# Residual laid into the PSUM accumulators ahead of the output projection, in a two-layer hybrid decoder trunk with routed experts

## The chip, the cores and the metric

One NeuronCore of one Trainium2 chip runs the whole program. The metric is the device time of one execution in microseconds, lower is better. Times of groups of runs are given as their median.

## What is computed

The input x has 256 tokens of 1024 float32 values. There are two layers, each a token mixer and then a channel mixer, with RMS norms ahead and residual additions behind. Cut to what matters:

```python
for layer in range(2):
    h = rms_norm(x, norm_mix_g[layer])
    mix = even_mixer(h, ...) if layer % 2 == 0 else odd_mixer(h, ...)   # both end in  o @ w_out
    x = x + mix
    h = rms_norm(x, norm_ffn_g[layer])
    x = x + hier_moe(h, ...)
```

Layer 0 mixes by differential attention (4 heads, whose outputs are normed once more) and stick-breaking attention (8 heads); layer 1 by attention with a forget gate (16 heads). In the channel mixer each token picks one of 4 groups and two of the 4 experts in it; an expert is `(silu(h @ w_gate) * (h @ w_up)) @ w_down` with three matrices of 1024 x 1024, so 12 MB of weights each, and there are 16 experts in each layer. All weights are float32.

## The kernel before, in words

The kernel is written engine by engine, each in an own program order, and the engines meet at semaphores. The residual stream x lies in SBUF as `x_sb`, 128 tokens by 2 by 1024. Its four quarters (q = 0 to 3) are token tile q // 2 and column half q % 2, 128 x 512 each, the size of one PSUM bank. There are eight banks: banks 0 to 3 are named `ACC`, 4 and 5 `GATE` and `UP`, 6 `Y` (also `O_BANK`), 7 `MISC` (also `SUM_BANK`).

**Attention and its end.** TensorE makes scores, transposes and weighted values for 8 jobs, in banks 0 to 6, and ScalarE copies each output into `oT` (L653), counted by `o_ready`. `exp_done` counts the exponentials that ScalarE has taken out of the score banks. In layer 0 VectorE and ScalarE then find the norms of the first four outputs; TensorE spreads them over the partitions in banks 0 and 1 (L1384) and VectorE multiplies (L1136), counted by `sub_applied`.

**Output projection.** TensorE goes through the four quarters, each with 8 float32 products of 128 x 512 (L1395), which the trace records as two passes each, into banks 2 to 5. After each quarter VectorE adds x to the bank and writes the sum to `x_sb` (L797), counted by `x_mixed`. ScalarE sums the squares (L713). TensorE transposes the quarters of the new x through the identity (L1188) into banks 0 to 3, the first two of them in the middle of the projection; VectorE takes them into `hT` with the norm's gain (L774).

**Router.** TensorE multiplies `hT` with the router's weights, in 8 chunks for each token tile (L1411, 20 columns each), into bank 7 and signals `logits_psum`. Then it copies the four quarters of `x_sb` through the identity into banks 0 to 3 (L1416, with start=True), so that the experts' outputs can be accumulated on the residual there, and waits for `chosen`. Meanwhile VectorE works out the choice of experts in some 20 small instructions (L960 to L992, `chosen_bf`), then makes `fn_low` of the second token tile (L812: the part of the normed rows that the rounded copy `fn_high` leaves out), and only then waits for the ranks, which TensorE makes from `chosen_bf` (L1425). From the ranks come slot numbers (L1000, L1003) and the 0/1 matrix `take` of the first expert (L1044).

**Experts.** For each expert TensorE gathers the tokens (L1435, 8 products of 512 columns), ScalarE takes them out (L725), TensorE transposes (L1445), VectorE takes these out (L1058), and then gate, up and down products follow (L1457, 64 columns by 512, in pairs on both halves of the array), in 6 units of 16 recorded passes for each expert. The output of each expert is scattered onto the accumulators (L1469). After the last one VectorE copies the four banks to `x_sb` (L1169).

**Weights.** SP issues all weight loads from one queue. An expert's weights are six units of 2 MB, in a ring of eight slots and a spare one that overlaps `hn` and `hT`. During attention the first expert's six units are loaded, behind them w_out. After the projection (`out_psum`) SP loads two units of the second expert, after the router (`logits_psum`) a third into the spare slot. Each further load waits until TensorE has used the slot (`unit_used`), in a fixed order; the first such refill waits for the first unit of the first expert.

## Time and profile before

| what | value |
|---|---|
| median of three runs | 1252.6 us |
| the three runs | 1251.89, 1252.60, 1255.09 us |
| the profiled execution, its own time | 1256.46 us |
| its span, from the first to the last instruction | 1254.5 us |
| mean granted TensorE clock, as a share of full | 0.984 |
| TensorE busy with products | 1174.7 us (94%) |
| VectorE, ScalarE, GpSimd busy | 423.6, 189.9, 7.2 us |
| read from HBM | 437.8 MB, 350 GB/s over the span |

Times in the profile are microseconds from the start of the span unless marked ns. Rows name an engine, a line of the kernel (L1395), an operation, what it writes and reads, shapes, and how often (x8). PE is TensorE's products, DVE VectorE, ACT ScalarE, SPq the queue of SP, that issues DMAs. In brackets stands how long the engine was idle before and what ended that. A float32 product appears as two records. PEclk is the clock granted to TensorE: 1.00 is 2.4 GHz, 0.50 is 1.2 GHz. Matmul ends are modelled, and rows that are merged are read from their start.

### The profile page before, as it was taken

How to read it: one execution, taken by the hardware profiler on the slowest of the kernel's cores; microseconds unless marked ns; L12 is line 12 of the kernel's file. 1: busy time of each engine (PE TensorE's matmuls, PEld its weight loads, DVE VectorE, ACT ScalarE, POOL GpSimd, SP SyncE). 2: the span in 40 equal slices, each digit the busy share in tenths (PEclk: the TensorE clock that was granted, in tenths of full speed). 3: DMA queues.
4: the chain of work that ended last, by engine and by line, in shares of the span. 5: the costliest groups of instructions: out<-in, count | busy, mean ns of one | idle time of the engine just before them, and what ended most of it. 6: DMA issues, size and time to landing. Idle time of an engine off the chain costs nothing.

```text
span 1254.5 us, 14037 instructions
## 1 busy us (share of the span) xinstructions
PE 1174.7 (94%) x5694; PEld 560.5 (45%) x5694; DVE 423.6 (34%) x748; ACT 189.9 (15%) x374; POOL 7.2 (1%) x36
## 2 busy tenths in 40 slices
PE   5997899999999999989979999999999999999998
PEld 4994453333333333333369864533333333333333
DVE  3654243232322232222255663433222323222223
ACT  3326210000000000000044242100000100000000
POOL 2000000000000000000000000000000000000000
PEclk9998889999999999999989999899999999999999
DMA  9665047999999999999994450699999999999996
GB/s 329 203 256 201 1 197 314 422 418 431 428 428 428 428 428 427 430 428 427 422 364 158 179 202 1 243 429 411 415 433 427 427 427 432 427 428 427 429 429 270
DMA packets 53904, 439.30 MB, mean 350 GB/s; under 512 B 14192, under 2 KB 14192, under 8 KB 29296
## 3 DMA queue, kind: packets, MB, share of 16 engines
q1 hardware_dynamic: 53872, 438.85, 84.5%
q8 instruction: 22, 0.36, 0.1%
q14 instruction: 10, 0.08, 0.0%
HBM read 437.79 MB, written 1.05 MB: 350 GB/s over the span
## 4 chain that ended last, share of the span: by engine, by line
PE 74%; DMA 17%; DVE 4%; ACT 3%; issue 1%; POOL 1%; DVEq 0%; POOLq 0%; SPq 0%; ACTq 0%
PE bank L1457 42%; DMA ring<-in_moe_w_up 11%; PE bank L1350 8%; DMA ring<-in_moe_w_gate 6%; PE bank L1395 5%; PE bank L1435 4%; PE bank L1469 4%; PE bank L1345 3%; PE bank L1445 1%; ACT attention L629 1%; PE bank L1501 1%; PE bank L1416 1%; PE bank L1188 1%; PE bank L1494 1%; PE bank L1282 1%
## 5 line engine op out<-in xcount | busy, mean ns | idle before, releaser
L1457 PE MATMUL bank<-ring,qkT 128*64 128x512 f32 x2944 | 655.0, 597 | 28.3 <-DMA ring<-in_moe_w_gate 15.5
L1457 PEld LDWEIGHTS bank<-ring,qkT 128*64 128x64 f32 x2944 | 204.8, 137 | 454.3 <-issue 406.6
L1152 DVE TENSOR_SCALAR qkT<-qkT 128x512 f32<-128x512 f32 x32 | 13.7, 428 | 486.4 <-ACT qkT L738 486.4
L1154 DVE RECIPROCAL qkT<-qkT 128x512 f32<-128x512 f32 x32 | 107.3, 3353 | 1.1
L1469 PE MATMUL bank<-qkT 64*128 64x512 f32 x256 | 63.6, 615 | 5.6 <-ACT qkT L743 5.6
L1159 DVE TENSOR_TENSOR qkT<-bank,qkT 128x512 f32<-128x512 f32 x32 | 22.1, 692 | 132.0 <-PE bank L1457 132.0
L743 ACT ACTIVATE qkT<-bank 128x512 f32<-128x512 f32 x32 | 19.1, 597 | 304.3 <-PE bank L1457 304.3
L1395 PE MATMUL bank<-ring,hn 128*128 128x512 f32 x128 | 57.3, 606 | 1.4 <-DVE hn L1136 0.8
L738 ACT ACTIVATE qkT<-bank 128x512 f32<-128x512 f32 x32 | 19.1, 598 | 243.2 <-PE bank L1457 243.2
L920 DVE TENSOR_TENSOR w_low<-ring,w_high 128x2048 fp32r<-128x2048 f32 x22 | 49.4, 2286 | 11.6 <-ACT w_high L586 11.6
L1435 PE MATMUL bank<-fn_high,take 128*128 128x512 f32 x136 | 45.9, 419 | 2.1 <-DVE take L1044 2.1
L741 ACT ACTIVATE qkT<-bank 128x256 f32<-128x256 f32 x32 | 12.3, 383 | 224.2 <-PE bank L1494 224.2
L1435 PE MATMUL bank<-fn_low,take 128*128 128x512 f32 x136 | 42.4, 393 | 0.0
L586 ACT ACTIVATE w_high<-ring 128x2048 fp32r<-128x2048 f32 x22 | 40.7, 1898 | 6.3 <-PE bank L1350 6.3
L1395 PEld LDWEIGHTS bank<-ring,hn 128*128 128x128 f32 x128 | 24.7, 196 | 31.9 <-issue 30.3
L1435 PEld LDWEIGHTS bank<-fn_high,take 128*128 128x128 f32 x136 | 22.9, 188 | 31.3 <-issue 28.2
L1469 PEld LDWEIGHTS bank<-qkT 64*128 64x128 f32 x256 | 22.0, 186 | 30.6 <-issue 15.1
L1350 PE MATMUL bank<-h_high,w_high 128*128 128x256 f32 x224 | 30.9, 291 | 0.0
L725 ACT ACTIVATE qkT<-bank 128x512 f32<-128x512 f32 x34 | 20.3, 597 | 62.8 <-PE bank L1435 62.8
L1457 PE MATMUL bank<-ring_spare,qkT 128*64 128x512 f32 x128 | 29.2, 598 | 0.0
L1350 PE MATMUL bank<-h_high,w_low 128*128 128x256 f32 x224 | 29.2, 283 | 0.0
L1350 PE MATMUL bank<-h_low,w_high 128*128 128x256 f32 x224 | 29.1, 283 | 0.0
(217 smaller groups left out, 898.3 us busy)
## 6 DMA issues: line engine op xcount, KB each, us to landing
ring<-in_moe_w_gate SPq DMA_DIRECT2D x64, 2048.0 KB, 22.2
ring<-in_moe_w_down SPq DMA_DIRECT2D x64, 2048.0 KB, 24.9
ring<-in_moe_w_up SPq DMA_DIRECT2D x56, 2048.0 KB, 24.4
ring_spare<-in_moe_w_up SPq DMA_DIRECT2D x8, 2048.0 KB, 26.5
ring<-in_ab_w_in SPq DMA_DIRECT2D x12, 1024.0 KB, 14.2
ring<-in_c_w_in SPq DMA_DIRECT2D x12, 1024.0 KB, 14.4
ring<-in_ab_w_out SPq DMA_DIRECT2D x2, 2048.0 KB, 15.1
ring<-in_c_w_out SPq DMA_DIRECT2D x2, 2048.0 KB, 15.3
```

The costliest lines, as they stand in the source:

```text
L586: act.activation(w_high[u % 2][:, part, :], win_view(u)[:, part, :], ACT.Copy).then_inc(s.w_high, 1)
L725: act.activation(gathered_sb, MISC[:, :], ACT.Copy).then_inc(s.gather_out, 1)
L738: act.activation(sig, GATE[:, :], ACT.Exp, scale=-1.0).then_inc(s.gate_exp, 1)
L920: tt(w_low[u][:, part, :], win_view(u)[:, part, :], w_high[u % 2][:, part, :].bitcast(F32), ALU.subtract).then_inc(s.w_low, 1)
L1154: nc.vector.reciprocal(sig, sig).then_inc(s.gate_step, 1)
L1159: tt(hid, UP[:, :], sig, ALU.mult).then_inc(s.hid_ready, 1)
L1345: last = mm(bank[j % 2][:, :], x_part[:, c, P * t:P * (t + 1)], w[:, c, :], start=(n == 0 and c == 0), stop=(final and c == NC - 1))
L1350: last = mm(bank[j % 2][:, T * half:T * (half + 1)], w[:, c, col:col + P], x_part[:, c, :], start=(n == 0 and half == 0 and c == 0), stop= ...
L1395: last = mm(bank[2 + q][:, :], oT[:, c, P * t:P * (t + 1)], wout_view(c // SUB)[:, c % SUB, HALF * h:HALF * (h + 1)], start=(c == 0), stop ...
L1435: last = mm(MISC[:, :], take[:, t, side:side + P], part[:, t, HALF * h:HALF * (h + 1)], start=(t == 0 and i == 0 and h == 0), stop=(t == N ...
L1457: last = mm(b[SLOTS * half:SLOTS * (half + 1), :], left(h, k), expert_rhs(slot, k, half), start=(h == 0 and k == 0), stop=(h == 1 and k == ...
L1469: last = mm(ACC[2 * t + half][:, :], giveT[k % 2][r, P * t:P * (t + 1)], y_sb[r, :], start=False, stop=False, skip_group_check=True)
```

## The change

The residual goes into banks 0 to 3 ahead of the output projection, and the projection is accumulated on it there. VectorE copies the sum to `x_sb` where it added. The copies through the identity behind the router are gone, and the transposes of the new x go to banks 4, 5, 6 and again 4. Of the copies, those of quarters 2 and 3 (into banks 2 and 3) are issued after the last exponential has been taken out, in layer 0 ahead of the spreading of the norms, and those of quarters 0 and 1 behind the wait for all attention outputs. The fourth group of transposes waits until VectorE has read the first out of bank 4.

```diff
--- before.py
+++ after.py
@@ -273,6 +273,7 @@
         bank = [ctx.enter_context(nc.psum_tensor(f"bank{i}", [P, COLS], F32)) for i in range(8)]
         ACC, GATE, UP, Y, MISC = bank[0:4], bank[4], bank[5], bank[6], bank[7]
         O_BANK, SUM_BANK = bank[6], bank[7]
+        MIXED_T = [bank[4], bank[5], bank[6], bank[4]]
 
 
         pool_step = sem("pool_step")
@@ -765,14 +766,14 @@
                 own(tt(tmp, tmp, ys, ALU.mult))
                 return stt(ys, tmp, 1.5, ys, ALU.add, ALU.mult)
 
-            def leave_transposed(layer, n, table, groups, first_bank):
+            def leave_transposed(layer, n, table, groups, banks):
 
                 s = layers[layer]
                 for g in groups:
                     t, h = g // 2, g % 2
                     dve.wait_ge(s.ht_psum, 8 * layer + 4 * n + g + 1)
                     tt(hT[:, SUB * h:SUB * (h + 1), P * t:P * (t + 1)],
-                       bank[first_bank + g][:, :].rearrange("p (c t) -> p c t", c=SUB),
+                       banks[g][:, :].rearrange("p (c t) -> p c t", c=SUB),
                        gains(table, layer, h, P), ALU.mult).then_inc(s.ht_ready, 1)
 
             def mix_norm(layer):
@@ -785,16 +786,16 @@
                        ).then_inc(s.hn_ready, 1)
                 if layer == 0:
                     dve.wait_ge(gains_loaded, GAINS)
-                leave_transposed(layer, 0, gain_mix, range(4), 2)
+                leave_transposed(layer, 0, gain_mix, range(4), bank[2:6])
 
             def mixed_and_normed(layer):
 
                 s = layers[layer]
 
-                def add(q):
+                def leave(q):
                     dve.wait_ge(s.out_psum, 4 * layer + q + 1)
                     xq = x_sb[:, q // 2, HALF * (q % 2):HALF * (q % 2 + 1)]
-                    tt(xq, bank[2 + q][:, :], xq, ALU.add).then_inc(s.x_mixed, 1)
+                    nc.vector.tensor_copy(xq, ACC[q][:, :]).then_inc(s.x_mixed, 1)
 
                 def norm(t):
                     xs, ys, tmp = root_x[:, t:t + 1], root_y[:, t:t + 1], root_t[:, t:t + 1]
@@ -812,18 +813,18 @@
                     stt(fn_low[:, t, :], x_sb[:, t, :], root_y[:, t:t + 1],
                         fn_high[:, t, :].bitcast(F32), ALU.mult, ALU.subtract).then_inc(rows_low, 1)
 
-                add(0)
-                add(1)
+                leave(0)
+                leave(1)
                 norm(0)
                 low(0)
                 for t in range(NT):
                     for side in (0, 2):
                         ts(take[:, t, SLOTS * side:SLOTS * (side + 1)], slot_id[:, 0, :], -1.0, None,
                            ALU.is_equal)
-                add(2)
-                leave_transposed(layer, 1, gain_ffn, (0, 1), 0)
-                add(3)
-                leave_transposed(layer, 1, gain_ffn, (2, 3), 0)
+                leave(2)
+                leave_transposed(layer, 1, gain_ffn, (0, 1), MIXED_T)
+                leave(3)
+                leave_transposed(layer, 1, gain_ffn, (2, 3), MIXED_T)
                 norm(1)
                 return low
 
@@ -1174,7 +1175,7 @@
         def _(pe):
             mm = nc.tensor.matmul
 
-            def tokens_across(layer, n, groups, first_bank):
+            def tokens_across(layer, n, groups, banks):
 
                 s = layers[layer]
 
@@ -1184,8 +1185,10 @@
                         pe.wait_ge(s.hn_ready, 4 * layer + t + 1)
                     else:
                         pe.wait_ge(s.x_mixed, 4 * layer + g + 1)
+                        if g == 3:
+                            pe.wait_ge(s.ht_ready, 8 * layer + 4 + 1)
                     for c in range(SUB):
-                        last = nc.tensor.transpose(bank[first_bank + g][:, P * c:P * (c + 1)],
+                        last = nc.tensor.transpose(banks[g][:, P * c:P * (c + 1)],
                                                    by_chunk((hn, x_sb)[n], t, h, c), ident[:, :])
                     last.then_inc(s.ht_psum, 1)
 
@@ -1292,7 +1295,7 @@
             pe.wait_ge(consts_made, CONSTS)
             for layer in range(LAYERS):
                 s = layers[layer]
-                tokens_across(layer, 0, range(4), 2)
+                tokens_across(layer, 0, range(4), bank[2:6])
                 pe.wait_ge(s.ht_ready, 8 * layer + 4)
                 if layer == 1:
                     pe.wait_ge(forget_loaded, FORGET)
@@ -1376,6 +1379,14 @@
                         across(layer, i - 1)
                     if layer == 0 and 3 <= i < 3 + SUBLN:
                         sub_sum(s, i - 3)
+                def residual(q):
+
+                    mm(ACC[q][:, :], ident[:, :], x_sb[:, q // 2, HALF * (q % 2):HALF * (q % 2 + 1)],
+                       start=True, stop=False, skip_group_check=True)
+
+                pe.wait_ge(s.exp_done, 2 * JOBS)
+                residual(2)
+                residual(3)
                 if layer == 0:
                     pe.wait_ge(s.root_done, 2)
                     for g in range(2):
@@ -1388,34 +1399,31 @@
                     pe.wait_ge(s.sub_applied, 2)
                 pe.wait_ge(wout_loaded, 32 * (layer + 1))
                 pe.wait_ge(s.o_ready, JOBS)
-                pe.wait_ge(s.exp_done, 2 * JOBS)
+                residual(0)
+                residual(1)
                 for q in range(4):
                     t, h = q // 2, q % 2
                     for c in range(NC):
-                        last = mm(bank[2 + q][:, :], oT[:, c, P * t:P * (t + 1)],
-                                  wout_view(c // SUB)[:, c % SUB, HALF * h:HALF * (h + 1)], start=(c == 0),
-                                  stop=(c == NC - 1))
+                        last = mm(ACC[q][:, :], oT[:, c, P * t:P * (t + 1)],
+                                  wout_view(c // SUB)[:, c % SUB, HALF * h:HALF * (h + 1)], start=False,
+                                  stop=False, skip_group_check=True)
                     last.then_inc(s.out_psum, 1)
                     if q == 2:
-                        tokens_across(layer, 1, (0, 1), 0)
+                        tokens_across(layer, 1, (0, 1), MIXED_T)
 
                 if layer == 0:
                     pe.wait_ge(router_loaded, ROUTER)
-                tokens_across(layer, 1, (2,), 0)
+                tokens_across(layer, 1, (2,), MIXED_T)
                 for i in range(NT):
                     for h in range(2):
                         if i == 1 and h == 0:
-                            tokens_across(layer, 1, (3,), 0)
+                            tokens_across(layer, 1, (3,), MIXED_T)
                         pe.wait_ge(s.ht_ready, 8 * layer + 4 + 2 * i + h + 1)
                         for c in range(SUB * h, SUB * (h + 1)):
                             last = mm(MISC[:, NR * i:NR * (i + 1)], hT[:, c, P * i:P * (i + 1)],
                                       w_rt[:, layer, c, :], start=(c == 0), stop=(c == NC - 1))
                 last.then_inc(logits_psum, 1)
 
-                for q in range(4):
-                    last = mm(ACC[q][:, :], ident[:, :],
-                              x_sb[:, q // 2, HALF * (q % 2):HALF * (q % 2 + 1)], start=True,
-                              stop=False, skip_group_check=True)
                 pe.wait_ge(chosen, layer + 1)
 
                 ranks = [(0, [(before_bf, 0)]), (1, [(ones_bf, 0), (before_bf, 1)]),
```

## Rows read from the trace of the kernel before

**Rows 1.** The page's span, and its DMA row in 40 slices.

```profile
span 1254.5 us, 14037 instructions
...
DMA  9665047999999999999994450699999999999996
```

**Rows 2.** The chain that ended last: start us, length us, what.

```profile
184.65 2.10 PE bank L1435 x8
...
581.48 35.42 DMA ring<-in_moe_w_up
...
634.13 1.29 DVE x_sb L1169 x2
```

**Rows 3.** Windows of the refills; columns: length, busy of PE, PEld, DVE, ACT, POOL, PEclk, DMA share, GB/s.

```profile
195.20:617.00 421.80, 406.59 (x1862) 153.27 (x1859) 115.24 (x153) 33.82 (x62) 0.00 (x0) 1.00 1.00 426
810.60:1233.00 422.40, 407.01 (x1862) 153.37 (x1858) 115.23 (x153) 33.83 (x62) 0.00 (x0) 1.00 1.00 425
```

**Rows 4.** Timeline of SP's queue, both layers: start us, length us, what.

```profile
172.07 0.82 SPq L423 DMA_DIRECT2D ring<-in_moe_w_gate  x2
...
195.22 0.37 SPq L423 DMA_DIRECT2D ring<-in_moe_w_up  x1
...
810.56 0.35 SPq L423 DMA_DIRECT2D ring<-in_moe_w_up  x1
```

**Rows 5.** Timeline at the end of layer 1, VectorE.

```profile
1249.24 2.48 DVE L1169 COPY x_sb<-bank 128x512 f32<-128x512 f32 x4 [9.55 <-PE bank L1469]
```

**Rows 6.** Timeline of layer 0, end of attention to the projection.

```profile
135.66 0.87 PE L1282 MATMUL bank<-attention,v_sb 128*64 128x256 f32 x8 [0.95 <-ACT hn L653]
...
137.64 3.37 PE L1384 MATMUL bank<-root_y,ident 32*128 32x256 f32 x8 [1.10 <-DVE root_y L766]
...
141.05 0.75 DVE L1136 SCALAR_TENSOR_TENSOR hn<-hn,g_sub,bank 128x512 f32<-128x512 f32 x1 [0.96 <-PE bank L1384]
...
141.85 22.37 PE L1395 MATMUL bank<-ring,hn 128*128 128x512 f32 x48 [0.84 <-DVE hn L1136]
```

**Rows 7.** Timeline of layer 1, end of attention to the projection.

```profile
759.52 0.87 PE L1282 MATMUL bank<-attention,v_sb 128*64 128x256 f32 x8 [0.70 <-DVE attention L906]
...
760.91 20.84 PE L1395 MATMUL bank<-ring,hn 128*128 128x512 f32 x48 [0.52 <-issue]
```

**Rows 8.** Lines L797 and L1098: count, ns min/median/max, starts, shapes.

```profile
L797 DVE TENSOR_TENSOR x_sb<-bank,x_sb x8: 691/692/692, 150.5 to 789.6; 128x512 f32<-128x512 f32 x8
...
L1098 DVE COPY qkT<-bank x14: 682/691/692, 27.3 to 699.8; 128x512 f32<-128x512 f32 x14
```

**Rows 9.** Timeline of layer 0, routing to the first expert.

```profile
177.21 6.28 PE L1416 MATMUL bank<-x_sb,ident 128*128 128x512 f32 x8
...
180.90 1.28 DVE L812 SCALAR_TENSOR_TENSOR fn_low<-x_sb,root_y,fn_high 128x1024 fp32r<-128x1024 f32 x1
...
183.64 0.19 DVE L1000 SCALAR_TENSOR_TENSOR attention<-bank,chosen_bf 128x32 f32<-128x32 f32 x1 [1.47 <-PE bank L1425]
...
189.04 8.78 PE L1457 MATMUL bank<-ring,qkT 128*64 128x512 f32 x32 [0.87 <-DVE qkT L1058]
```

**Rows 10.** Timeline of layer 1, routing to the first expert.

```profile
798.11 1.28 DVE L812 SCALAR_TENSOR_TENSOR fn_low<-x_sb,root_y,fn_high 128x1024 fp32r<-128x1024 f32 x1
...
801.18 0.19 DVE L1000 SCALAR_TENSOR_TENSOR attention<-bank,chosen_bf 128x32 f32<-128x32 f32 x1 [1.79 <-PE bank L1425]
...
806.56 7.09 PE L1457 MATMUL bank<-ring,qkT 128*64 128x512 f32 x32 [0.86 <-DVE qkT L1058]
```

**Rows 11.** Windows around the low clock; columns as in rows 3.

```profile
142.00:144.90 2.90, 2.90 (x4) 1.35 (x5) 0.00 (x0) 0.00 (x0) 0.00 (x0) 0.50 0.00 0
175.50:182.40 6.90, 6.90 (x15) 3.83 (x15) 4.78 (x24) 1.76 (x4) 0.00 (x0) 0.51 1.00 427
189.20:192.70 3.50, 3.50 (x10) 1.04 (x10) 2.46 (x15) 0.00 (x0) 0.00 (x0) 0.51 0.02 5
800.20:810.00 9.80, 7.21 (x35) 3.49 (x35) 5.62 (x34) 0.69 (x2) 0.00 (x0) 1.00 0.59 251
```

## The prediction

> **What bounds the kernel now.** I read the page first: of the span of 1254.5 us the DMA row stands at 9 over nearly all of both expert stages and falls to 0 in the attention ahead of each [rows 1]. So the question is who waits for whom at the end of an expert stage. The chain of waits answers: late in layer 0 it runs for 35.42 us over the load of an expert unit, not over TensorE [rows 2]. The windows confirm it: from the first refill of the weight ring to near the end of the stage, the DMA engines are busy with share 1.00 at 425 to 426 GB/s in both layers, while TensorE has some 15 us of gaps in each [rows 3]. The refills begin when the queue of SP sees the first ring slot freed, which is when TensorE has used the first unit of the first expert: at 195.22 us in layer 0 and 810.56 us in layer 1 [rows 4]. From there to the end of the last copy out of the accumulators it is 635.42 - 195.22 = 440.2 us in layer 0 and 1251.72 - 810.56 = 441.2 us in layer 1 [rows 2, 5]. The two agree within 1 us. An expert stage is therefore a fixed length of transfer behind one event, and whatever moves this event moves the end by as much. Ahead of it the DMA engines are idle or have only the three units loaded at 172.07 us and after, so these loads hide nothing and cost nothing here. The working below is the shift of the first refill in each layer, and the two shifts add.
>
> **The change part by part.** I take the path in order of time, in each layer. The moved work is eight copies through the identity, each of two passes of 512 columns. In a long row at the high clock a pass takes 0.43 us: the 48 passes of the output projection in layer 1 take 20.84 us [rows 7]. The same 48 passes in layer 0 took 22.37 us [rows 6], 1.53 us more, since the first of them ran at a granted clock of 0.50 [rows 11]. A pair of copies is four passes: 1.72 us high, 3.44 us low.
>
> *Layer 0, quarters 2 and 3.* TensorE has finished the last attention product at 135.66 + 0.87 = 136.53 us and starts L1384 at 137.64 us [rows 6]. The idle 1.11 us takes most of the pair: **+0.6 us**. If the pair runs at the low clock it is 3.44 - 1.11 = +2.3. If the added work keeps the clock high under L1384 (3.37 us [rows 6]) that group halves, and the term is 0.6 - 1.7 = -1.1. I take +0.6, since L1384 is small work and before it the engine stands idle either way.
>
> *Layer 0, quarters 0 and 1.* They stand behind the wait for L1136, which ends at 141.05 + 0.75 = 141.80 us; the projection started at 141.85 us [rows 6]. Nothing hides this pair: **+1.7 us**. It may run at the low clock, but then the projection's first passes, low so far, do not.
>
> *Layer 1.* The last attention product ends at 759.52 + 0.87 = 760.39 us and the projection starts at 760.91 us [rows 7]. Both pairs come in between: 760.39 + 3.44 = 763.83, so **+2.9 us**, 0.5 us of it hidden. Above, 6.9 us at the low clock, +6.4; below, nothing less than 2.9 as the clock is high there already.
>
> *The projection and what leaves it.* The number of products is the same. VectorE now copies where it added: the addition from PSUM took 691 to 692 ns, and a copy of the same shape from PSUM takes 682 to 692 ns [rows 8], so **0**. The transposes go to banks 4 to 6. The new wait of the fourth group is on VectorE's reading of bank 4, which is over one quarter of the projection (7 us) earlier, so 0. Behind it in TensorE's queue stand the router's products of the second half. The three loads that SP issues after the projection shift with it and are still done before the first refill, as now: 0.
>
> *Routing.* L1416 starts at 177.21 us and lasts 6.28 us. The choice of experts is ready in the meantime, but VectorE then makes the low half of the rows (L812, 180.90 + 1.28 = 182.18 us) ahead of the ranks, and waits for TensorE until 183.64 us [rows 9]. Without L1416 the rank products are done under L812. What the removal gives back is only this wait, 1.46 us, less the 0.05 us from one instruction of VectorE to the next: **-1.4 us**, and in layer 1 (801.18 - 799.39 = 1.79) **-1.8 us** [rows 10]. So of 6.3 us taken away four fifths were beside VectorE's work.
>
> *What L1416 did besides.* The granted clock tells why it took 6.3 us and not 3.4: it was low from 175.5 to 182.4 us, and rose only after L1416 had kept the array streaming for over 5 us [rows 11]. The gather of the first tokens, 1.0 us after VectorE's ranks, then ran high. Without L1416, TensorE has the router's products of 20 columns and then some 5 us with almost nothing, and meets the gather at the low clock. It lasts 2.1 us [rows 2]; doubled but for the 0.2 us by which a last pass ends late, **+1.9 us** in each layer, +0.1 us for the four transposes behind it (small, estimated by the same doubling with most of their time being latency). Bounds 0 and +2.1. The Trainium skill (TensorE: Matmul & The Clock Gate, section Part 1) puts it so: "the default state is throttled, and activity releases the throttle"; by this rule the identity copies paid for their place, and the trace agrees [rows 11], while a count of instructions alone would give -1.4 and -1.8 here and no penalty.
>
> *First expert.* Its first 32 products took 8.78 us in layer 0, where the clock fell again at 189.2 us, and 7.09 us in layer 1, where it stayed high [rows 9 to 11]. The difference is 1.7 us. I take such a low stretch for both: **0** in layer 0, which has it, and **+1.7 us** in layer 1. Bounds: -1.7 and +1.7 in layer 0; 0 and +3.5 in layer 1 (the whole first unit low).
>
> **Sum.** Layer 0: 0.6 + 1.7 - 1.4 + 1.9 + 0.1 + 0 = +2.9. Layer 1: 2.9 - 1.8 + 1.9 + 0.1 + 1.7 = +4.8. Together +7.7 us. The profiled execution took 1256.5 us (span 1254.5), 3.9 us over the median of the three runs, which is within what the low stretches of the clock can move (1.5 to 1.7 us each). Set against the median: 1252.6 + 7.7 = **1260.3 us**.
>
> **Rivals.**
> 1. *The clock charges nothing.* Gather and first expert run high. For it: the clock fell only near 175.5 us [rows 11], over 3 us after the projection, behind which SP issues at 172.07 us [rows 4], so it bears small work for a while. Against it: the small work and the idle time are longer than that now. Sum: 0.6 + 1.7 - 1.4 + 2.9 - 1.8 = +2.0, so 1254.6 us. Chance 0.18.
> 2. *Not slower: the clock never falls.* One mechanism, from L1384 to the first expert: copies placed into the idle time keep the clock high. Layer 0: -1.1 for the first pair, +1.7, -1.5 for the projection's first passes, -1.4, -1.7 for the first expert: -4.0. Layer 1: 2.9 - 1.8 = +1.1. Sum -2.9, so 1249.7 us. It decides if the granted clock is 1.00 at L1384 and at the gather. Against it: the copies are far ahead of the routing, where the idle time grows. Chance 0.05.
> 3. *More low clock.* The first pair at the low clock (+1.7 over my term) and low first units in both layers (+1.7, +1.8): 7.7 + 5.2 = 12.9, so 1265.5 us. Chance 0.12.
> 4. *Routing was the bound after all*: L1416 delays the chain by its full length. Then -6.3 twice, +1.7 + 0.6 + 2.9, -7.4 us: 1245.2. VectorE's L812 before the ranks speaks flatly against it. Chance 0.01.
>
> **How the numbers follow.** The forecast has the rest, 0.64: 1260.3 us. The range takes in rival 1 and comes near rival 3: 1254.4 to 1265.3. A measurement here can tell about 0.3%, 3.8 us. Slower by more: the forecast, rival 3, and little of rival 1: 0.76. Within: most of rival 1, a part of the forecast with a cheaper gather, and half of rival 2: 0.20. Faster, the rest of rival 2 and rival 4: 0.04.
>
> **What the profile would show.** Right: L1395 starts 2 to 3 us later than before against the end of attention in both layers; VectorE goes from L812 straight to the ranks; the granted clock is 0.5 under the first gather, which lasts near 4 us; the first refill of layer 0 some 3 us and of layer 1 some 8 us later than before; 440 to 441 us from each to the end of its stage. Wrong: a granted clock of 1.00 under the gather (rival 1), a shorter layer 0 up to the router (rival 2), or stages that do not keep their length, in which case the DMA reasoning falls.

## The result and the profile after

The changed kernel took 1260.46 us (median of 5 runs, 1258.3 to 1262.1), the kernel before 1252.34 us beside it: a ratio of 1.0064 with a 95% interval of 1.0046 to 1.0082, 8.1 us slower. On a second occasion it was 1261.39 against 1251.99 us, 1.0065 (1.0041 to 1.0088). The forecast was 1260.3 us, 7.7 us over the 1252.6 us of the three earlier runs.

The page of the changed kernel, to be laid beside [rows 1]; the second row is the granted clock, in tenths:

```profile
span 1258.5 us, 14038 instructions
...
PEclk9998989999999999999999999799999999999999
...
DMA  9665048999999999999994350699999999999996
```

The picture is that of before, 4 us longer. The chain of waits (start us, length us, what) still goes through a load near the end of layer 0, and SP's queue (the same three events as in [rows 4]) gives the first refills:

```profile
581.27 35.42 DMA ring<-in_moe_w_up
...
633.94 1.29 DVE x_sb L1170 x2
```

```profile
171.29 0.83 SPq L424 DMA_DIRECT2D ring<-in_moe_w_gate  x2
...
193.92 0.37 SPq L424 DMA_DIRECT2D ring<-in_moe_w_up  x1
...
813.55 0.35 SPq L424 DMA_DIRECT2D ring<-in_moe_w_up  x1
```

From the first refill to the end of the last copy it is 635.23 - 193.92 = 441.3 us in layer 0 (before 440.2 [rows 2, 4]). The last copies of layer 1 end at 1255.72 us, 442.2 us after its first refill (before 441.2 [rows 4, 5]). So each expert stage kept its length within 1.1 us, and the DMA engines are still busy with share 1.00 from the first refill to near the end of the stage, as the last two of these windows show (length, busy of PE, PEld, DVE, ACT, POOL, granted clock, DMA share, GB/s):

```profile
140.00:143.00 3.00, 3.00 (x4) 1.01 (x3) 0.00 (x0) 0.00 (x0) 0.00 (x0) 0.50 0.00 0
...
177.30:190.80 13.50, 7.97 (x25) 4.37 (x27) 8.20 (x45) 0.69 (x2) 0.00 (x0) 0.50 0.78 333
...
795.20:812.00 16.80, 10.17 (x29) 4.91 (x31) 9.55 (x54) 1.64 (x4) 0.00 (x0) 0.50 0.69 295
...
193.90:617.00 423.10, 407.06 (x1862) 153.33 (x1860) 115.24 (x153) 33.85 (x62) 0.00 (x0) 1.00 1.00 425
...
813.60:1236.00 422.40, 406.49 (x1860) 153.28 (x1856) 114.92 (x153) 33.83 (x62) 0.00 (x0) 1.00 1.00 425
```

The second and third windows are the ones that matter. The granted clock is at 0.50, that is 1.2 GHz, for 13.5 us and for 16.8 us from behind the router into the first expert. Before, in layer 0, it was low for 6.9 us at the same place, under most of L1416, and for 3.5 us more under the first expert [rows 11].

The timeline of layer 0 (start us, length us, engine, line, operation, what, count; lines have moved: L1384 are now the copies, L1395 the spreading of the norms, L1407 the projection, L1423 the router, L1443 the gather, L1465 the experts), against [rows 6, 9]:

```profile
133.61 0.87 PE L1285 MATMUL bank<-attention,v_sb 128*64 128x256 f32 x8 [0.94 <-ACT hn L654]
...
134.41 1.98 PE L1384 MATMUL bank<-x_sb,ident 128*128 128x512 f32 x4
...
136.33 1.99 PE L1395 MATMUL bank<-root_y,ident 32*128 32x256 f32 x8
...
139.16 3.27 PE L1384 MATMUL bank<-x_sb,ident 128*128 128x512 f32 x4 [0.84 <-DVE hn L1137]
...
142.22 21.22 PE L1407 MATMUL bank<-ring,hn 128*128 128x512 f32 x48
...
173.81 2.02 PE L1423 MATMUL bank<-w_rt,hT 128*128 128x20 f32 x16
...
179.38 1.28 DVE L813 SCALAR_TENSOR_TENSOR fn_low<-x_sb,root_y,fn_high 128x1024 fp32r<-128x1024 f32 x1
...
180.58 0.18 DVE L1001 SCALAR_TENSOR_TENSOR attention<-bank,chosen_bf 128x32 f32<-128x32 f32 x1
...
181.58 1.19 PE L1443 MATMUL bank<-fn_high,take 128*128 128x512 f32 x2 [1.76 <-DVE take L1045]
...
184.27 1.05 PE L1443 MATMUL bank<-fn_low,take 128*128 128x512 f32 x2
...
188.01 8.51 PE L1465 MATMUL bank<-ring,qkT 128*64 128x512 f32 x32 [0.87 <-DVE qkT L1059]
```

And of layer 1, against [rows 7, 10]:

```profile
757.38 0.87 PE L1285 MATMUL bank<-attention,v_sb 128*64 128x256 f32 x8 [0.70 <-DVE attention L907]
...
758.18 3.70 PE L1384 MATMUL bank<-x_sb,ident 128*128 128x512 f32 x8
...
761.72 20.76 PE L1407 MATMUL bank<-ring,hn 128*128 128x512 f32 x48
...
798.39 1.28 DVE L813 SCALAR_TENSOR_TENSOR fn_low<-x_sb,root_y,fn_high 128x1024 fp32r<-128x1024 f32 x1
...
799.59 0.18 DVE L1001 SCALAR_TENSOR_TENSOR attention<-bank,chosen_bf 128x32 f32<-128x32 f32 x1
...
807.02 9.61 PE L1465 MATMUL bank<-ring,qkT 128*64 128x512 f32 x32 [0.86 <-DVE qkT L1059]
```

What is to be seen. In layer 0 the first pair of copies ran at the high clock (1.98 us), filled the idle time, and the spreading of the norms then took 1.99 us instead of 3.37 us; the second pair met the low clock (3.27 us). The projection starts 142.22 - 134.48 = 7.7 us after the end of attention, 5.3 us before. In layer 1 both pairs took 3.5 us and the projection starts 3.5 instead of 0.5 us after it. VectorE goes from the low rows (L813) to the ranks (L1001) without waiting, in both layers. The gather lasts from 181.58 us to 185.32 us, 3.7 us, where it was 2.1 us [rows 2]. The first 32 expert products took 8.51 and 9.61 us.

The sum of what happened between the end of attention and the first refill: 58.7 us before and 59.4 us after in layer 0, 50.2 and 55.3 us in layer 1, so 5.9 us. The two stages of this execution are 2.1 us longer than those of the profile before. That is no more than such lengths vary: in the eight profiles of kernels with no extra work behind the first refill, the sixteen stages took 439.9 to 442.2 us, and the changed kernel's on the second occasion 440.6 and 441.6 us. That the profiled executions differ by 4.0 us only is due to 2.0 us in each attention, ahead of what was changed: in layer 0 attention ended at 134.48 us instead of 136.53 us with the same instructions. A single execution of this kernel isn't a fair measure: over the study the kernel before ran between 1246.4 and 1258.0 us.

### The profile page after: what moved, and what is told of

The parts are those of the page before. It is cut to its first block, busy times and chain, and to the rows that moved or that the text cites. A ratio compares the mean times of both kernels' runs of the same rounds, so it can differ in the third digit from the quotient of the medians.

```text
span 1258.5 us, 14038 instructions
## 1 busy us (share of the span) xinstructions
PE 1169.7 (93%) x5694; PEld 556.9 (44%) x5694; DVE 423.1 (34%) x748; ACT 189.8 (15%) x374; POOL 7.2 (1%) x36
## 3 DMA queue, kind: packets, MB, share of 16 engines
HBM read 437.79 MB, written 1.05 MB: 349 GB/s over the span
## 4 chain that ended last, share of the span: by engine, by line
PE 68%; DMA 23%; DVE 4%; ACT 3%; issue 1%; POOL 1%; DVEq 0%; POOLq 0%; SPq 0%; ACTq 0%
PE bank L1465 37%; DMA ring<-in_moe_w_gate 12%; DMA ring<-in_moe_w_up 11%; PE bank L1353 8%; PE bank L1407 4%; PE bank L1443 4%; PE bank L1477 4%; PE bank L1348 3%; ACT attention L630 1%; PE bank L1453 1%; PE bank L1509 1%; PE bank L1285 1%; PE bank L1191 1%; PE bank L1502 1%; PE bank L1384 1%
## 5 line engine op out<-in xcount | busy, mean ns | idle before, releaser
L1465 PE MATMUL bank<-ring,qkT 128*64 128x512 f32 x2944 | 657.7, 598 | 29.9 <-DMA ring<-in_moe_w_gate 16.5
L1465 PEld LDWEIGHTS bank<-ring,qkT 128*64 128x64 f32 x2944 | 205.1, 137 | 458.7 <-issue 409.0
L1153 DVE TENSOR_SCALAR qkT<-qkT 128x512 f32<-128x512 f32 x32 | 13.7, 428 | 490.1 <-ACT qkT L739 490.1
L1407 PE MATMUL bank<-ring,hn 128*128 128x512 f32 x128 | 56.0, 596 | 0.0
L921 DVE TENSOR_TENSOR w_low<-ring,w_high 128x2048 fp32r<-128x2048 f32 x22 | 49.4, 2286 | 11.6 <-ACT w_high L587 11.6
L1443 PE MATMUL bank<-fn_high,take 128*128 128x512 f32 x136 | 47.8, 434 | 3.5 <-DVE take L1045 3.5
L1443 PE MATMUL bank<-fn_low,take 128*128 128x512 f32 x136 | 44.1, 406 | 0.0
L1443 PEld LDWEIGHTS bank<-fn_high,take 128*128 128x128 f32 x136 | 23.8, 195 | 32.9 <-issue 26.0
L1407 PEld LDWEIGHTS bank<-ring,hn 128*128 128x128 f32 x128 | 24.5, 193 | 30.5 <-issue 30.5
L1443 PEld LDWEIGHTS bank<-fn_low,take 128*128 128x128 f32 x136 | 26.7, 196 | 6.4
L1465 PE MATMUL bank<-ring_spare,qkT 128*64 128x512 f32 x128 | 29.2, 598 | 0.0
L1353 PE MATMUL bank<-h_high,w_low 128*128 128x256 f32 x224 | 29.2, 283 | 0.0
```

Source lines behind the costliest of these rows:

```text
L921: tt(w_low[u][:, part, :], win_view(u)[:, part, :], w_high[u % 2][:, part, :].bitcast(F32), ALU.subtract).then_inc(s.w_low, 1)
L1353: last = mm(bank[j % 2][:, T * half:T * (half + 1)], w[:, c, col:col + P], x_part[:, c, :], start=(n == 0 and half == 0 and c == 0), stop= ...
L1407: last = mm(ACC[q][:, :], oT[:, c, P * t:P * (t + 1)], wout_view(c // SUB)[:, c % SUB, HALF * h:HALF * (h + 1)], start=False, stop=False, ...
L1443: last = mm(MISC[:, :], take[:, t, side:side + P], part[:, t, HALF * h:HALF * (h + 1)], start=(t == 0 and i == 0 and h == 0), stop=(t == N ...
L1465: last = mm(b[SLOTS * half:SLOTS * (half + 1), :], left(h, k), expert_rhs(slot, k, half), start=(h == 0 and k == 0), stop=(h == 1 and k == ...
```

## Experiments

The two halves of the change are work put ahead of the projection and work taken from behind the router. The theory was that each has a price, and that the second is paid in clock; the rival that the clock is incidental and all of the loss lies ahead of the projection. All kernels were timed beside the kernel before; differences to it in us are the ratio, less 1, times 1252. The recorded ratio is not always the quotient of the two medians; the two differ by up to 0.2%. Distances "after attention" are counted from the end of the layer's last attention product, in the one profiled execution of each kernel.

### The changed kernel as reference

> The changed kernel once more, beside the three that follow, as their reference on the same chip. Theory: ratio to the kernel before near 1.0064 (8 us).

Measured: 1.0065, as told above. First refills 59.5 and 55.6 us after the end of attention (59.4 and 55.3 in the first profile), clock low for 13.7 and 17.1 us behind the router again, in another execution whose attention ended 2.4 us later. So two executions out of two show these long stretches.

### Unread copies back behind the router

```diff
+                def fill(q):
+
+                    mm(bank[4 + q % 2][:, :], ident[:, :],
+                       x_sb[:, q // 2, HALF * (q % 2):HALF * (q % 2 + 1)], start=True, stop=True,
+                       skip_group_check=True)
+
+                for q in range(4):
+                    fill(q)
                 pe.wait_ge(chosen, layer + 1)
```

> The changed kernel, and behind the router four copies through the identity into banks 4 and 5 that nobody reads, as many as the kernel before had there. Theory (about half of the loss is the clock): gather back to about 2.1 us and the first expert's first 32 products to 7 to 9 us, which gives back 3 to 4 us per layer, while VectorE waits 1.4 to 1.8 us for the ranks again; 3 to 5 us faster than the changed kernel in all, so 3 to 5 us slower than before. Rival (the clock costs nothing, all of the loss is the work put ahead of the projection): the fill only adds the wait, 3 us slower than the changed kernel, some 11 us slower than before.

Measured: 1254.26 against 1251.99 us, 1.0012 (0.9995 to 1.003), so 7.1 us faster than the changed kernel by the medians, with 16 passes per execution more on TensorE. Gather 2.1 us, the first 32 products 7.09 us, in both layers. The rival fails. My own figure, 3 to 5 us, was too small by 2 us or more: it charged waits of 1.4 to 1.8 us for the ranks, and the profile has none in layer 0 and 0.55 us in layer 1. First refills: 56.0 and 51.4 us after the end of attention.

### Unread copies sized to the idle time

```diff
+                fill(0)
+                fill(1)
                 pe.wait_ge(chosen, layer + 1)
...
                 last.then_inc(rank_psum, 1)
+                fill(2)
```

> The changed kernel with three such unread copies, sized to the idle time: two behind the router and one behind the rank products. Theory: they delay nothing (VectorE goes from L813 straight to the ranks) and keep the array streaming, so that the clock is high again from the gather or the first expert on; 4 to 7 us faster than the changed kernel, 1 to 4 us slower than before. Rival (the clock costs nothing): the same as the changed kernel.

Measured: 1256.54 us, 1.0037 (1.0018 to 1.0055), 4.9 us faster than the changed kernel (95% interval from their single times: 2 to 7 us) and 4.6 us slower than before, a little over the 1 to 4 us expected. This is the cleanest run on the clock, because nothing but TensorE's idle time is touched: ranks and gather of both layers begin at the same distance from the end of attention as in the changed kernel, to 0.02 us. Timeline of TensorE and the window of the low clock in it, layer 0:

```profile
175.94 1.96 PE L1429 MATMUL bank<-x_sb,ident 128*128 128x512 f32 x4
...
179.92 1.10 PE L1429 MATMUL bank<-x_sb,ident 128*128 128x512 f32 x2
...
184.54 0.69 PE L1452 MATMUL bank<-fn_low,take 128*128 128x512 f32 x2
...
187.53 7.09 PE L1474 MATMUL bank<-ring,qkT 128*64 128x512 f32 x32 [0.86 <-DVE qkT L1059]
```

```profile
181.30:184.70 3.40, 2.86 (x7) 2.32 (x8) 1.84 (x14) 0.00 (x0) 0.00 (x0) 0.50 1.03 436
```

The clock fell all the same, but for 3.4 us and not 13.5. It still covers most of the gather (its last row is already 0.69 us, not 1.05) and is high again for the transposes and the first expert, whose first 32 products take 7.09 us instead of 8.51. In layer 1 the gather took 2.9 us and the first 32 products 7.09 us instead of 9.6 to 9.9. The first refills came at 57.3 and 51.5 us, 2.2 and 3.8 us sooner than in the first profile of the changed kernel.

### The early copies alone

```diff
+                pe.wait_ge(s.exp_done, 2 * JOBS)
+                early(2)
+                early(3)
                 if layer == 0:
                     pe.wait_ge(s.root_done, 2)
...
-                pe.wait_ge(s.exp_done, 2 * JOBS)
+                early(0)
+                early(1)
```

> The kernel before, with the change's four copies ahead of the projection as additional, unused work, and all else as before. Theory: 0.6 + 1.7 us in layer 0 and 2.9 us in layer 1, so 5 us slower than before, between 3 and 7. Rival (the clock costs nothing, so the whole loss of 8 us plus the 3 us that routing gained came from here): 11 us slower than before.

Measured: 1253.17 us, 1.0007 (0.999 to 1.0025): 1 us slower, at most 3. Both expectations (5, between 3 and 7, and 11 us) were too high. The path did lengthen as worked out, with the projection ending 1.3 us later after attention in layer 0 (the start is 2.8 us later, but the first 48 passes are faster by the clock) and 2.9 us later in layer 1. It is given back behind the router. These are the copies of layer 0, those of layer 1, and VectorE's ranks in layer 1:

```profile
177.65 3.68 PE L1425 MATMUL bank<-x_sb,ident 128*128 128x512 f32 x8
...
796.18 5.38 PE L1425 MATMUL bank<-x_sb,ident 128*128 128x512 f32 x8
...
801.71 0.19 DVE L1000 SCALAR_TENSOR_TENSOR attention<-bank,chosen_bf 128x32 f32<-128x32 f32 x1 [0.57 <-PE bank L1434]
```

L1425 here is what L1416 is in the kernel before: 3.68 us in layer 0, at the high clock, and 5.38 us in layer 1, in part at the low one, against 6.28 us in layer 0 before [rows 9]. So the wait for the ranks is 0 in layer 0 and 0.57 us in layer 1, where it was 1.47 and 1.79 us [rows 9, 10]. First refills: 56.0 and 51.4 us, within 0.02 us the same as with the four unread copies behind the router, which puts TensorE's work in the same places. The two differ in the rest of the change, VectorE's copy where it added and the other banks, so these cost nothing that the refills show.

### Early copies in layer 0 only

```diff
                 if layer == 0:
+                    pe.wait_ge(s.exp_done, 2 * JOBS)
+                    early(2)
+                    early(3)
                     pe.wait_ge(s.root_done, 2)
...
+                if layer == 0:
+                    early(0)
+                    early(1)
```

> The kernel before with the four early copies as unused work in layer 0 only. With them in both layers the first refill of layer 0 came 2.7 us earlier after the end of attention than before, and that of layer 1 1.2 us later. If the early copies pay for themselves by the clock in layer 0: 1 to 3 us faster than before. If that was the luck of one execution: 1 to 2.4 us slower.

Measured: 1250.18 against 1250.64 us, 0.9991 (0.9972 to 1.0009). The interval reaches from 3.5 us faster to 1.1 us slower: a loss of 2 us is out, a gain of 1 to 3 us is neither shown nor excluded. The first refill of layer 0 came 55.9 us after attention as with both; in layer 1, without early copies, 47.8 us, where the same work took 50.2 us in the profile before. There the clock stayed high from the router to the first refill, L1416 took 3.68 us, and VectorE did not wait for the ranks.

### Control: the loop's first pass written out

```diff
-                with pe.Fori(0, last_quad + 1) as quad:
+                one_quad(0, True)
+                with pe.Fori(1, last_quad + 1) as quad:
+                    one_quad(quad, False)
```

> Control for the next two: the kernel before with TensorE's first pass of the expert loop written out ahead of the loop, the same work in the same order. Expected by every theory: within 1 us of before.

Measured: 0.9987 (0.9969 to 1.0005), 1251.35 against 1250.64 us. The form of the loop costs nothing that can be seen, so the next kernels can be read. Its expert stages are 441.1 and 440.5 us, its first refills 55.2 and 50.8 us after attention: 3.5 us sooner in layer 0 than in the profile of before, with the same work. So much do these distances vary by the clock. In layer 1 the control had bad luck: its projection ended 31.5 us after attention, where the other kernels without early copies have 29.2 us, since it ran partly at the low clock.

### The removal alone, copies behind the gate units

```diff
-                for q in range(4):
-                    last = mm(ACC[q][:, :], ident[:, :],
...
                         two_halves(GATE, tokens, quad, k, (0, 1))
+                        if inside and k == 0:
+                            for q in range(4):
+                                residual(q)
```

> The kernel before (first loop pass written out) with L1416's four copies moved out of the routing gap to behind the first two units of the first expert; nothing ahead of the projection. It is the change's removal by itself. Theory (the copies paid for their place by the clock, and behind the first refill work is free): VectorE waits for no ranks, -1.4 and -1.8 us, but gather +1.7 and first expert low, +2 to +3 us per layer; 1 to 6 us slower than before. Rival (the clock costs nothing): 3.2 us faster.

Measured: 1258.77 us, 1.0058 (1.0037 to 1.0079), 7 us slower, more than either expected. The first refills came at 56.6 and 52.4 us, 3.0 us later in sum than in the control (5.3 us, if the 2.4 us of the control's slow projection are taken off); but the stages also grew, they were 443.3 and 443.6 us. The windows of layer 0 behind its first refill at 191.07 us show why:

```profile
195.90:201.90 6.00, 6.00 (x26) 2.89 (x26) 2.94 (x2) 0.60 (x1) 0.00 (x0) 1.00 1.01 434
...
201.90:205.90 4.00, 4.00 (x20) 1.15 (x16) 0.00 (x0) 0.00 (x0) 0.00 (x0) 1.00 0.67 205
```

TensorE makes the copies from 193.59 us on (3.70 us). The third refill is then issued at 202.88 us, 11.8 us after the first one where the control has 8.4 us, and the DMA share falls to 0.67 for 4 us. The expectation that behind the first refill TensorE's work is free was wrong.

### The same behind the up units, and in the second expert's turn

Here too L1416's four copies are taken out behind the router, and the first pass of the loop is written out; only the lines that put them back are shown.

```diff
                         two_halves(UP, tokens, quad, k, (2, 3))
+                        if inside and k == 0:
+                            for q in range(4):
+                                residual(q)
```

> As the kernel with all four copies behind the first expert's gate units, but behind its up units instead, so that the third refill isn't held back. That kernel's expert stages had grown from 440 to 442 us to 443.4 and 443.7 us, with the DMA engines idle for some 1.3 us while TensorE made the copies ahead of the units whose slots come free next. Theory: stages back to 440 to 442 us, low clock under the gather as before, 2 to 5 us slower than the kernel before. Rival (the copies cost by the clock alone, wherever they stand): 8 us slower, as that one.

```diff
                         if k >= 1:
+                            if inside and k == 1:
+                                for q in range(4):
+                                    residual(q)
                             scatter(turns(quad, k), k - 1)
```

> All four copies moved out of the routing gap to just ahead of the first scatter, in the second expert's turn, some 45 us behind the first refill; nothing ahead of the projection. This is the removal by itself, without copies in the first turn, where they had lengthened the expert stage by 2 to 3 us. Theory A (the two halves of the change add up): early copies alone cost 1 us, so the removal alone must cost 7 to 8 us, at the first refills, with stages of 440 to 442 us. Theory B (they do not add: the early copies shift where the clock falls and make the low stretch after the router longer): stages 440 to 442 us, the low clock ends sooner than 13 us after it began, and the removal alone costs 0 to 4 us. Rival (clock free): 3.2 us faster.

Measured: 1258.42 us, 1.0053 (1.0035 to 1.0071), and 1260.38 us, 1.0053 (1.0034 to 1.0073). The stages stayed at 442.9 to 443.6 us in both, so the expectation of 440 to 442 us failed twice: even in the second turn the four copies (some 3.4 us) hold back a refill until the loads run dry. Both kernels are 6.6 us slower than before, between the theory's 2 to 5 us and the rival's 8 us for the first of them. The first refills came at 56.5 and 49.8 us with the copies behind the up units. SP's queue and the windows of the kernel with the copies in the second turn, layer 0:

```profile
195.47 0.36 SPq L423 DMA_DIRECT2D ring<-in_moe_w_up  x1
...
243.19 3.74 SPq L423 DMA_DIRECT2D ring<-in_moe_w_gate  x2
```

```profile
236.00:240.00 4.00, 4.00 (x16) 1.40 (x16) 0.00 (x0) 0.00 (x0) 0.00 (x0) 1.00 1.00 426
...
240.00:242.00 2.00, 2.00 (x12) 0.66 (x10) 0.00 (x0) 0.00 (x0) 0.00 (x0) 1.00 0.64 270
...
242.00:244.00 2.00, 2.00 (x12) 0.64 (x10) 0.00 (x0) 0.00 (x0) 0.00 (x0) 1.00 0.02 8
...
244.00:246.00 2.00, 2.00 (x12) 0.72 (x10) 0.00 (x0) 0.00 (x0) 0.00 (x0) 1.00 1.00 254
```

From 240 to 244 us the DMA engines lose some 2.7 us. In the kernel before that refill is issued at 239.52 us, 44.3 us after the first one, here 47.7 us after. Taking the stages' growth over the control (442.9 + 443.4 - 441.1 - 440.5 = 4.7 us) from 6.6 us leaves about 2 us for the removal itself, which is within what theory B gave; theory A asked for 7 to 8 us at the first refills, and the profile has 59.0 and 49.8 us after attention, 2.7 us in sum over the control, or 5.1 us with the control's slow projection taken off. But theory B's second mark, a shorter low stretch, came in layer 1 (10.2 us) and not in layer 0 (17.1 us). The figure of 2 us is a difference and was not measured by itself; the refills of the three kernels allow 2 to 5 us.

### Splitting the copies over the gap

Two copies stand behind the router, one behind the rank products. The fourth stands, in three kernels, behind the first expert's gate units (shown), behind its up units, or ahead of the first scatter, in the second turn.

```diff
-                for q in range(4):
-                    last = mm(ACC[q][:, :], ident[:, :],
...
+                residual(0)
+                residual(1)
                 pe.wait_ge(chosen, layer + 1)
...
                 last.then_inc(rank_psum, 1)
+                residual(2)
...
+                        if inside and k == 0:
+                            for q in (3,):
+                                residual(q)
```

> The same, but the residual copies of quarters 0 and 1 stand behind the router, that of quarter 2 behind the rank products, and only that of quarter 3 behind the first two units. Theory: ranks wait for nothing, the array streams through the gap, gather at 2.1 us in most executions; 2 to 5 us faster than before. If the clock stays low under the gather in spite of three copies: 0 to 3 us slower. Rival (the clock costs nothing): 3.2 us faster, the same as with all four moved.

> Two copies behind the router, one behind the rank products, the fourth behind the first expert's up units; nothing ahead of the projection. Theory: first refills as with the fourth behind the gate units (55 and 48 us after the end of attention) and stages of 441 instead of 443 us, so 2 to 5 us faster than before. If the stages were only unlucky there: the same as before.

> Two copies behind the router, one behind the rank products, the fourth just ahead of the first scatter. The same layout with the fourth copy in the first turn was the same as before in time. Theory: first refills 1 to 3 us earlier than before and stages of 440 to 442 us; 0 to 3 us faster than before, perhaps within the spread.

Measured, with the fourth copy behind the gate units: 1252.25 us, 1.0002 (0.9983 to 1.0021), stages 443.1 and 442.4 us. Behind the up units: 1252.17 us, 1.0001 (0.9983 to 1.0019), stages 440.8 and 440.9 us. Ahead of the first scatter: 1249.48 against 1253.44 us, 0.9971 (0.9956 to 0.9986), stages 440.5 and 441.0 us. The first two were expected 2 to 5 us faster than before, and both failed that. In the second the stages did come back to 441 us, and yet it was level with before. The third was expected 0 to 3 us faster. It is 3.6 us faster than before and, by the ratios, 11 to 12 us faster than the change. Since its near twin was level with before, on another occasion, I take from it that the layout is no slower, and that a gain of a few us was seen once. First refills: 54.9 and 47.8, 55.0 and 48.3, 55.4 and 48.2 us. Layer 1 of it:

```profile
791.06 3.76 PE L1417 MATMUL bank<-x_sb,ident 128*128 128x512 f32 x4
...
794.68 1.28 DVE L812 SCALAR_TENSOR_TENSOR fn_low<-x_sb,root_y,fn_high 128x1024 fp32r<-128x1024 f32 x1
...
794.98 2.05 PE L1417 MATMUL bank<-x_sb,ident 128*128 128x512 f32 x2
...
795.88 0.19 DVE L1000 SCALAR_TENSOR_TENSOR attention<-bank,chosen_bf 128x32 f32<-128x32 f32 x1
...
801.20 7.09 PE L1461 MATMUL bank<-ring,qkT 128*64 128x512 f32 x32 [0.78 <-DVE qkT L1058]
```

The ranks follow L812 at once, the third copy fits between them and the gather, and the gather meets the high clock; the first 32 products take 7.09 us. So VectorE's wait for the ranks is gone, as in the change, and the clock is high for the gather and the first expert.

## Why the prediction was right, and where its parts were not

The time was right, 1260.3 against 1260.5 us; that it fits to 0.2 us is luck, since the median of the changed kernel alone moved by 0.9 us from one occasion to the other, and errors of 1 us and more in the terms cancelled. The mechanism was right in its main parts: a first refill behind which the stage keeps its length, copies laid ahead of the projection onto the path, a routing gap in which L1416 had mostly stood beside VectorE, and the clock that it had brought up for the gather. But the split between the terms was off. Step by step, against the profiled kernel before:

| step | forecast us | measured us |
|---|---|---|
| layer 0, early copies, to the start of the projection | +2.3 | +2.4 |
| layer 0, projection's first 48 passes | 0 | -1.2 |
| layer 1, early copies | +2.9 | +3.0 |
| router's products, layers 0 and 1 | 0 | -0.8, -0.5 |
| wait for the ranks, layers 0 and 1 | -1.4, -1.8 | -1.5, -1.8 |
| gather, each layer | +1.9 | +1.7 |
| from gather to first expert, each | +0.1 | +0.4 |
| first expert to first refill, layers 0 and 1 | 0, +1.7 | -0.3, +2.5 |
| to the first refill, both layers | +7.7 | +5.9 |
| stages, both (first profile; +0.8 on the second occasion) | 0 | +2.1 |

**The early copies.** In layer 1 they lie on the path as forecast, to 0.1 us. In layer 0 the +2.4 us to the start of the projection agree with the forecast by luck. The first pair was taken at +0.6 us; in fact it ran high and kept the clock high under the spreading of the norms, so that the second pair starts 139.16 - 134.48 = 4.7 us after attention, where the projection started 5.3 us after it before: -0.6 us. That is the case the prediction had put at -1.1 and rejected because "L1384 is small work"; it is the step that failed. The second pair was taken at +1.7 us and took 3.1 us at the low clock, and the projection gave 1.2 us of that back, as the sentence "the projection's first passes, low so far, do not" had it: +1.9 us in sum. So the projection of layer 0 ends 1.3 us later and not 2.3. Missing in the sum is what the copies do farther on: with L1416 still behind the router they cost 1 us in all and not 5.2 us.

**The routing.** VectorE no longer waits, as said, and the gain of 1.5 and 1.8 us against the profiled execution is there. But that execution had L1416 at the low clock. Where L1416 ran high throughout (3.68 us, layer 0 with early copies and layer 1 with early copies in layer 0 only) the wait is 0; in the control, where it took 5.13 and 5.38 us, it is 0.3 and 0.6 us. The term was read from one execution and taken as the kernel's.

**The clock.** The forecast charged 1.9 + 0.1 us per layer and 1.7 us once. From the kernel with the early copies alone to the changed kernel, whose one difference that takes time is L1416's copies, the first refill comes 3.5 us later in layer 0 and 3.9 to 4.2 us in layer 1, and the medians are 8.2 us apart. Of these, by the two profiles: gather 1.7 and transposes with their waits 0.4 us in each layer, first expert 1.4 and 2.5 us, less 0.6 us of the wait for the ranks in layer 1. Taken in this order, the early copies first, the early copies cost 1 us instead of 5.2 and the removal some 7.5 us instead of 2.5, and the two errors cancel. The split depends on the order: taken the other way, the removal first costs 2 to 5 us by the kernels with the copies moved behind the first refill, and the early copies the rest of the 8 us, which is nearer to the forecast's 2.5 and 5.2. What the runs do show is that the early copies change, through the clock, terms that the forecast took as fixed: L1416's length, the waits for the ranks and the first expert.

**Rival 1** (the clock charges nothing) is refuted by the unread copies: they take back 4.9 us where they delay nothing, 7.1 us where they stand as L1416 had. **Rival 2** (the clock never falls) was right on the first pair and nearly on L1395 in layer 0, but the clock fell under the second pair and was 0.50 under the gather. **Rival 3** had its long low stretches and, in layer 1, the longer first expert (+2.5 us), but the first pair ran high and the first expert of layer 0 was not longer than before. **Rival 4** has no support: with the wait gone, nothing like 6.3 us came back.

**The lengths of the stages.** The bound held for the change, whose added work lies ahead of the refill. The reason given was too strong: the stage is a fixed length of transfer only as long as TensorE frees the slots in time, and in the first two turns it does so with less to spare than the 3.4 us of four copies.

**What stays open.** Whether the halves add up. Early copies alone cost about 1 us (up to 3), the removal alone 2 to 5 us, both 8 us. The stretch from the end of the router's products to the first refill shows the pattern. With the four copies in it, it took 14.1 to 14.9 us in eight stretches of four kernels, and 17.8 and 15.9 us in the profile before, where L1416 ran low. With three copies in it, one of them behind the rank products, and the fourth behind the first refill, it took 14.0 to 14.5 us in six. With none in it and none early it took 15.4 to 18.6 us in six, and with none in it and four early, which is the change, 18.1 to 19.0 us in four. That the early copies make the low stretch behind the router longer would explain it: it was 13.5 to 17.1 us in both profiles of the changed kernel, and 10.2 to 17.1 us in the three without early copies. Six stretches against four don't settle it, and why the early copies should do this was not tested.

## What to carry to other kernels

Ahead of removing work from an engine's idle time, look at the granted clock under it and behind it: work that costs nothing can be what makes the next, critical products run at full rate, and its removal is then paid for there. Where a stage is bound by a ring of loads, cost every edit by the first event that lets the ring move, and don't take what is behind that event for free until the slack is measured. Terms that depend on the clock should be read from several executions, or from their bounds, not from the one profiled.

## What the runs showed of the hardware that was not expected

- The clock stayed low for 13.5 us in layer 0 and 16.8 us in layer 1 of the changed kernel, though the gather streams for 3.7 us inside it. The Trainium skill (TensorE: Matmul & The Clock Gate, section Why this matters for your kernels) advises to leave TensorE no long idle gaps between bursts of matmuls. The trace agrees: three unread copies in these gaps cut the low stretch of layer 0 to 3.4 us and took 4.9 us of the loss away.
- The same kernel's executions are spread over 11.6 us (1246.4 to 1258.0 us for the kernel before). Two profiles with the same work up to the end of attention in layer 0 had it at 134.5 and 136.5 us.
- Four copies of 3.4 us in all, moved into the first or second expert's turn, made an expert stage of 441 us 2 to 3 us longer, though TensorE has some 15 us of gaps in the stage as a whole [rows 3].
